# Feed-forward products of the prompt rows by Strassen's scheme, up phase before down phase

## The reference

```python
def _mlp(h, w_up, w_down):
    a = jnp.square(jax.nn.relu(jnp.einsum('bsd,df->bsf', h, w_up)))
    return jnp.einsum('bsf,fd->bsd', a, w_down)
# per layer: x = x + mixer(rmsnorm(x)) ; x = x + _mlp(rmsnorm(x), w_up, w_down)
```

## Time and profile before

| | |
|---|---|
| Median of 3 runs | 3071.8 us (3071.26 to 3075.94) |
| Profiled execution: time / span | 3069.31 / 3067.5 us |
| TensorE busy, products | 2958.7 us (96%) |
| TensorE busy, weight loads | 2498.5 us (81%) |
| VectorE, ScalarE, GpSimd busy | 1193.2, 907.5, 453.4 us |
| DMA | 165.91 MB, mean 54 GB/s |
| Mean granted TensorE clock | 0.987 |

### The profile page before, as it was taken

The page is one execution under the profiler, slowest core; times in us unless marked ns, Lnnn a source line. Parts: engine busy times, 40 slices in busy tenths (PEclk is TensorE's granted clock), DMA queues, the critical chain, the costliest instruction groups (busy, mean ns, idle before and its releaser), DMA issues.

```text
span 3067.5 us, 41859 instructions
## 1 busy us (share of the span) xinstructions
PE 2958.7 (96%) x16566; PEld 2498.5 (81%) x16566; DVE 1193.2 (39%) x2555; ACT 907.5 (30%) x1834; POOL 453.4 (15%) x283
## 2 busy tenths in 40 slices
...
DMA packets 146912, 165.91 MB, mean 54 GB/s; under 512 B 20032, under 2 KB 117600, under 8 KB 146784
## 3 DMA queue, kind: packets, MB, share of 16 engines
...
## 4 chain that ended last, share of the span: by engine, by line
PE 91%; DVE 5%; ACT 2%; issue 2%; POOL 1%; DMA 0%; ACTq 0%; SPq 0%; DVEq 0%; POOLq 0%
PE ps L1410 22%; PE ps L1408 22%; PE ps L1409 22%; PE ps L1550 6%; PE ps L1603 4%; PE ps L1580 4%; PE ps L1665 1%; PE ps L1522 1%; PE ps L1734 1%; PE ps L1420 1%; ACT pbuf L918 1%; DVE pbuf L1230 1%; POOL w_lo L698 1%; DVE pbuf L1198 1%; PE ps L1502 0%
## 5 line engine op out<-in xcount | busy, mean ns | idle before, releaser
L698 POOL TENSOR_TENSOR w_lo<-w_raw,w_hi 128x1024 fp32r<-128x1024 f32 (+2 forms) x158 | 376.4, 2383 | 2221.8 <-ACT w_hi L773 2221.8
L1408 PE MATMUL ps<-hT_hi,w_hi 128*128 128x384 f32 x1536 | 515.0, 335 | 4.8 <-DVE w_lo L1078 4.8
L1410 PE MATMUL ps<-hT_hi,w_lo 128*128 128x384 f32 x1536 | 514.6, 335 | 0.0
L1409 PE MATMUL ps<-hT_lo,w_hi 128*128 128x384 f32 x1536 | 514.4, 335 | 0.0
L1410 PE MATMUL ps<-w_hi,aT_lo 128*128 128x512 f32 x1152 | 448.4, 389 | 0.0
L1409 PE MATMUL ps<-w_lo,aT_hi 128*128 128x512 f32 x1152 | 448.4, 389 | 0.0
L1408 PE MATMUL ps<-w_hi,aT_hi 128*128 128x512 f32 x1152 | 448.1, 389 | 0.0
L1034 ACT ACTIVATE rbuf<-ps 128x384 f32<-128x384 f32 x192 | 94.5, 492 | 1140.9 <-PE ps L1410 1140.9
L1381 DVE TENSOR_TENSOR x<-ps,x 128x512 f32<-128x512 f32 x288 | 199.2, 692 | 560.2 <-PE ps L1410 560.2
L1373 DVE TENSOR_TENSOR rbuf<-rbuf 128x384 f32<-128x384 f32 x192 | 117.4, 612 | 577.1 <-ACT aT_hi L1036 577.1
L1408 PEld LDWEIGHTS ps<-hT_hi,w_hi 128*128 128x128 f32 x1536 | 289.4, 188 | 5.8 <-DVE w_lo L1078 5.3
...
## 6 DMA issues: line engine op xcount, KB each, us to landing
w_raw<-in_w_up_dram SPq DMA_DIRECT2D x64, 512.0 KB, 4.0
w_raw<-in_w_down_dram SPq DMA_DIRECT2D x64, 512.0 KB, 3.3
residual_scratch<-x SPq DMA_DIRECT2D x18, 512.0 KB, 7.7
x<-residual_scratch SPq DMA_DIRECT2D x18, 512.0 KB, 5.9
w_raw<-in_w_in_dram SPq DMA_DIRECT2D x16, 512.0 KB, 4.9
mixer_scratch<-omixT SPq DMA_DIRECT2D x16, 512.0 KB, 2.6
w_raw<-in_w_out_dram SPq DMA_DIRECT2D x16, 512.0 KB, 6.7
mixin<-mixer_scratch SPq DMA_DIRECT2D x16, 512.0 KB, 9.0
```

Source lines behind the costliest of these rows:

```text
L698: nc.gpsimd.tensor_tensor(w_lo[slot][:, 0:w], raw[i % 2][:, 0:w], w_hi[slot][:, 0:w], ALU.subtract).then_inc(lo_done.sem, 1)
L1408: pe.matmul(out, ah, bh, start=(k == 0), stop=False)
L1409: pe.matmul(out, ah, bl, start=False, stop=False)
L1410: last = pe.matmul(out, al, bh, start=False, stop=(k == n - 1))
```

## The change

Only the feed-forward changes (and, in its layout alone, the buffer of h for the other stages). The 8 x 8 grid of work over 1024 prompt rows is cut in halves in each dimension, and each of the 2x2 block products is made with Strassen's scheme in Winograd's form: 7 products of half size in place of 8, on sums and differences of the quarters of both operands. The 128 stream rows are multiplied in full.

- The layer first makes all hidden features (8 up turns), stores them in DRAM (`hidden_scratch`), and then makes all 8 down turns, loading them back. x goes to `residual_scratch2` before the up phase and is loaded back for the down phase, because T2, T3 and T4 (differences of the quarters of h, made once a layer) lie in its place.
- An up turn takes 256 features of each half. Its eight weight operands are the quarters 11, 12, 21, 22 and the sums S1 to S4, formed by VectorE, rounded by ScalarE, subtracted by GpSimd, in four slots. Its units (0, 1, 2, 3, 4, 6, 7) accumulate in PSUM; between them ScalarE copies partial results from PSUM to `cq`, VectorE adds the others to them, and squares with relu in one instruction. Four stream parts multiply 128 columns each.
- A down turn has nine weight operands (quarter 22 twice, and T1 to T4 formed by GpSimd) and eight hidden operands (the stream rows, quarters, S1 to S4 formed by VectorE), rounded by ScalarE; GpSimd makes the low parts of the weights, VectorE those of the hidden operands (`down_a_low`). TensorE makes first the stream products, then units 1 to 7, each in two pairs of tiles; VectorE adds each pair of banks (128 x 1024) into x, some results into two places by later units.
- `x_done` now tells of tiles 0 to 3, 4 and 5, and 6 to 8 only at the last two units of the last down turn.

The core of the diff (12 columns of indentation taken off; ScalarE's list and the T sums left out):

```diff
-FSLAB = 512
-NSLAB = FF // FSLAB
+NS = 8
+FB = FF // 2 // NS
...
+UP_OPS = ("11", "12", "S2", "S1", "S3", "21", "22", "S4")
+UP_END = (2, 5, 7, 9, 11, 12, 15, 17)
+UP_FREED_BY = (4, 5, 6, 7, 1, 1, 2, 3)
+UP_MM, UP_EV, UP_ADD = 17, 9, 3
...
+DN_B = ("22", "12", "11", "21", "T2", "T1", "T3", "22", "T4")
+DN_A = ("11", "12", "S1", "S2", "S3", "S4", "22")
+B_SLOT = (0, 1, 2, 3, 4, 0, 1, 2, 4)
+A_SLOT = (0, 1, 3, 2, 0, 1, 2)
+DN_MM = DN_EV = 15
...
-return dn_ev.at(l * NSLAB, 2 * (t + 1) - 18)
+return dn_ev.at(l * NS, (0 if t == NPT else 12 + t // 2) - DN_EV)
...
+    def down_turn(s):
+        T = l * NS + s
+        sp.wait_ge(a_lo.sem, a_lo.at(T, 1))
+        sp.wait_ge(a_out[4].sem, a_out[4].at(T, 32))
+        load(ras[:], as_d[s + 1], a_in[4])
+        sp.wait_ge(b_form.sem, b_form.at(T, 1))
+        sp.wait_ge(b_lo.sem, b_lo.at(T, 3))
+        load_down("11", s + 1)
+        sp.wait_ge(a_form.sem, a_form.at(T, 3))
+        sp.wait_ge(a_lo.sem, a_lo.at(T, 2))
+        for q in (0, 2):
+            sp.wait_ge(a_out[q].sem, a_out[q].at(T, 32))
+            load(ra[q][:], a_d[s + 1, q], a_in[q])
+        sp.wait_ge(b_form.sem, b_form.at(T, 3))
+        load_down("12", s + 1)
+        sp.wait_ge(b_form.sem, b_form.at(T, 4))
+        load_down("21", s + 1)
+        sp.wait_ge(a_form.sem, a_form.at(T, 4))
+        sp.wait_ge(a_out[1].sem, a_out[1].at(T, 32))
+        load(ra[1][:], a_d[s + 1, 1], a_in[1])
+        sp.wait_ge(b_lo.sem, b_lo.at(T, 8))
+        load_down("22", s + 1)
+        sp.wait_ge(a_lo.sem, a_lo.at(T, 8))
+        sp.wait_ge(a_out[3].sem, a_out[3].at(T, 32))
+        load(ra[3][:], a_d[s + 1, 3], a_in[3])
...
+    def down_low(T, o):
+        pool.wait_ge(b_hi.sem, b_hi.at(T, o + 1))
+        k = B_SLOT[o]
+        nc.gpsimd.tensor_tensor(wq_lo[k][:], down_b_source(o)[:], wq_hi[k][:],
+                                ALU.subtract).then_inc(b_lo.sem, 1)
+    def down_sums_12(T, s):
+        W = 2 * NS * l + NS + s
+        for q in (0, 1):
+            pool.wait_ge(wr_in[q].sem, wr_in[q].at(W, 16))
+        nc.gpsimd.tensor_tensor(bsum[0][:], rq[1][:], rq[0][:], ALU.subtract).then_inc(b_form.sem, 1)
+        pool.wait_ge(wr_in[3].sem, wr_in[3].at(W, 16))
+        pool.wait_ge(b_form.sem, b_form.at(T, 1))
+        nc.gpsimd.tensor_tensor(bsum[1][:], rq[3][:], bsum[0][:], ALU.subtract).then_inc(b_form.sem, 1)
+    def down_sum_3(T):
+        pool.wait_ge(b_lo.sem, b_lo.at(T, 6))
+        pool.wait_ge(b_form.sem, b_form.at(T, 2))
+        nc.gpsimd.tensor_tensor(bsum[0][:], rq[3][:], rq[1][:], ALU.subtract).then_inc(b_form.sem, 1)
+    def down_sum_4(T, s):
+        pool.wait_ge(b_lo.sem, b_lo.at(T, 5))
+        pool.wait_ge(wr_in[2].sem, wr_in[2].at(2 * NS * l + NS + s, 16))
+        nc.gpsimd.tensor_tensor(bsum[1][:], rq[2][:], bsum[1][:], ALU.subtract).then_inc(b_form.sem, 1)
...
+        down_low(T0, 0)
+        down_low(T0, 1)
+        down_low(T0, 2)
+        pool.wait_ge(up_mm.sem, up_mm.at(T, UP_END[4]))
+        down_sums_12(T0, 0)
+        down_low(T0, 3)
+        down_low(T0, 4)
...
+    def down_turn(T, s, last):
+        down_low(T, 5)
+        down_sum_3(T)
+        down_sum_4(T, s)
+        down_low(T, 6)
+        down_low(T, 7)
+        down_low(T, 8)
+        if not last:
+            down_low(T + 1, 0)
+            down_sums_12(T + 1, s + 1)
+            for o in range(1, 5):
+                down_low(T + 1, o)
...
+    def up_block(T, unit, copied, first_bank, q, k):
+        dve.wait_ge(up_mm.sem, up_mm.at(T, unit))
+        dve.wait_ge(up_ev.sem, up_ev.at(T, copied))
+        nc.vector.tensor_tensor(cq[q][:], bank(first_bank, 2), cq[q][:], ALU.add).then_inc(up_add.sem, 1)
+        dve.wait_ge(up_add.sem, up_add.at(T, k))
+        square(cq[q])
...
+    def down_a_low(T, o):
...
+        k = A_SLOT[o - 1]
+        nc.vector.tensor_tensor(sa_lo[k][:].rearrange("p k n -> p (k n)"), down_a_source(o - 1)[:],
+                                sa_hi[k][:].rearrange("p k n -> p (k n)"), ALU.subtract
+                                ).then_inc(a_lo.sem, 1)
...
+    def down_sums_12(T):
+        for q in (2, 3):
+            dve.wait_ge(a_in[q].sem, a_in[q].at(T, 16))
+        nc.vector.tensor_tensor(asum[0][:], ra[2][:], ra[3][:], ALU.add).then_inc(a_form.sem, 1)
+        dve.wait_ge(a_in[0].sem, a_in[0].at(T, 16))
+        dve.wait_ge(a_form.sem, a_form.at(T, 1))
+        nc.vector.tensor_tensor(asum[1][:], asum[0][:], ra[0][:], ALU.subtract).then_inc(a_form.sem, 1)
+    def down_sums_34(T):
+        dve.wait_ge(a_lo.sem, a_lo.at(T, 4))
+        dve.wait_ge(a_form.sem, a_form.at(T, 2))
+        nc.vector.tensor_tensor(asum[0][:], ra[0][:], ra[2][:], ALU.subtract).then_inc(a_form.sem, 1)
+        dve.wait_ge(a_in[1].sem, a_in[1].at(T, 16))
+        dve.wait_ge(a_lo.sem, a_lo.at(T, 5))
+        nc.vector.tensor_tensor(asum[1][:], ra[1][:], asum[1][:], ALU.subtract).then_inc(a_form.sem, 1)
+    def up_turn(T, s, first, last):
...
+        up_block(T, UP_END[0] + 2, 2, 4, 0, 1)
+        up_block(T, UP_END[3], 6, 2, 2, 2)
+        if not last:
+            dve.wait_ge(up_lo.sem, up_lo.at(T, 8))
+            up_sums_12(T + 1, s + 1)
+        dve.wait_ge(up_ev.sem, up_ev.at(T, 8))
+        square(cq[3])
+        dve.wait_ge(up_ev.sem, up_ev.at(T, 9))
+        square(cqs)
+        if last:
+            down_a_low(T0, 0)
+            down_a_low(T0, 1)
+            down_a_low(T0, 2)
+            down_sums_12(T0)
+        up_block(T, UP_END[7], 4, 2, 1, 3)
...
+    def evict(T, unit, pair, after):
+        half, t0 = ((0, 0), (0, 0), (1, 0), (1, 4), (1, 4), (1, 0), (0, 4))[unit - 1]
+        b0 = 4 if unit in (1, 3, 5, 7) else 0
+        dve.wait_ge(dn_mm.sem, dn_mm.at(T, 2 * unit + pair))
+        if after:
+            dve.wait_ge(dn_ev.sem, dn_ev.at(T, 2 * after + pair))
+        t = t0 + 2 * pair
+        part = x[:, t:t + 2, half * 512:(half + 1) * 512]
+        nc.vector.tensor_tensor(part, bank(b0 + 2 * pair, 2).rearrange("p (t n) -> p t n", t=2), part,
+                                ALU.add).then_inc(dn_ev.sem, 1)
+    def down_turn(T, last):
+        dve.wait_ge(dn_mm.sem, dn_mm.at(T, 1))
+        nc.vector.tensor_tensor(x[:, NPT, :], bank(0, 2), x[:, NPT, :], ALU.add).then_inc(dn_ev.sem, 1)
+        for unit in range(1, 8):
+            for pair in range(2):
+                evict(T, unit, pair, (0, 1, 0, 0, 4, 3, 0)[unit - 1])
+            if unit <= 3:
+                down_a_low(T, 4 + unit)
+            if last:
+                continue
+            if unit == 3:
+                down_a_low(T + 1, 0)
+            if unit == 4:
+                dve.wait_ge(a_lo.sem, a_lo.at(T, 8))
+                down_sums_12(T + 1)
+            if unit == 5:
+                down_a_low(T + 1, 1)
+            if unit == 6:
+                down_a_low(T + 1, 2)
+                down_a_low(T + 1, 3)
+            if unit == 7:
+                down_a_low(T + 1, 4)
+                down_sums_34(T + 1)
...
+    UNITS_UP = {0: (0, "11", True), 1: (4, "21", True), 2: (0, "T2", False), 3: (2, "T1", True),
+                4: (0, "T3", False), 6: (0, "T4", False), 7: (2, "22", False)}
+    def up_part(T, unit, fb, inc):
+        b0, name, new = UNITS_UP[unit]
+        wh, wl = wq_hi[unit % 4], wq_lo[unit % 4]
+        h, lo_h = H_HI[name], H_LO[name]
+        out = bank(b0 + fb)
+        for k in range(4):
+            cols = slice(k * FB + fb * P, k * FB + (fb + 1) * P)
+            pe.matmul(out, wh[:, cols], h[:, k, :], start=new and k == 0, stop=False, skip_group_check=True)
+            pe.matmul(out, wh[:, cols], lo_h[:, k, :], start=False, stop=False, skip_group_check=True)
+            last = pe.matmul(out, wl[:, cols], h[:, k, :], start=False, stop=k == 3, skip_group_check=True)
+        if inc:
+            last.then_inc(up_mm.sem, 1)
...
+        stream_part(0, 0, 0)
+        stream_part(1, 0, 4).then_inc(up_mm.sem, 1)
...
+    def down_products(out, ah, al, bh, bl, new, final):
+        for k in range(2):
+            pe.matmul(out, ah[:, k, :], bh[:, k * 512:(k + 1) * 512], start=new and k == 0, stop=False,
+                      skip_group_check=True)
+            pe.matmul(out, ah[:, k, :], bl[:, k * 512:(k + 1) * 512], start=False, stop=False,
+                      skip_group_check=True)
+            last = pe.matmul(out, al[:, k, :], bh[:, k * 512:(k + 1) * 512], start=False,
+                             stop=final and k == 1, skip_group_check=True)
+        return last
+    UNITS_DN = {1: (4, 1, 2, True), 2: (0, 2, 3, True), 3: (4, 4, 4, False), 4: (0, 3, 5, True),
+                5: (4, 5, 6, False), 6: (0, 6, 7, False), 7: (4, 7, 8, False)}
+    def down_turn(T):
+        pe.wait_ge(a_lo.sem, a_lo.at(T, 1))
+        pe.wait_ge(dn_ev.sem, dn_ev.at(T, 12 - DN_EV))
+        for o, half, k0 in ((0, 1, 2), (1, 1, 0), (2, 0, 0), (3, 0, 2)):
+            pe.wait_ge(b_lo.sem, b_lo.at(T, o + 1))
+            last = down_products(bank(half), sas_hi[:, k0:k0 + 2, :], sas_lo[:, k0:k0 + 2, :], wq_hi[o],
```

(27 more changed lines are left out.)

662 lines of the change are left out of this document (497 added, 165 removed).

## The result

The changed kernel takes 3127.01 us (median of 4, 3124.41 to 3128.53) beside 3071.53 for the kernel before on the same chip: a ratio of 1.0177, 95% interval 1.0164 to 1.019. It is slower, by 55.5 us; 3148 had been predicted, in a range of 3070 to 3210. The profiled execution took 3127.43 us, its span is 3125.6.

The account below looks back on a forecast made before the run. TensorE's products were taken to bound the kernel. Two layers +47.0, the next layer's start +0.5 and the end +28.5 made +76 us on 3069.31, and 2.5 more for the median gave 3148 us; range 3070 to 3210.

Parts of the forecast that it names:

- The likeliest case: Whole kernel slower through engine waits in down turns, pause between phases and longer tail; 3125 to 3170 us, chance 45%.
- the two engines' meetings: Down turns: VectorE instruction with two SBUF inputs waits until GpSimd's instruction ends; 3.3 us amid a string of GpSimd work.
- the gap: Between up and down phases: down products wait for VectorE's last addition, queued behind low parts and sums; 11.7 us a layer.
- the end: After the last product: final norm at GpSimd's 4.58 us pace, VectorE ending at 32.6 instead of 4.1; +28.5 us.
- Start of the phase: Before the first up product: ScalarE's square and copy, then two VectorE steps come last; 4.4 us a layer.
- The up phase: Eight up turns of 48.9 us, helper engines hidden; 391.1 us a layer, plus 1.8 stage transposes and 1.7 clock.
- the eight down turns with their clock: First turn 44.2 us, seven more of 50.7: 399.1 a layer, plus 13.6 for lowered clock after waits.
- the walk: Settled down turn timed by VectorE's instructions: TensorE waits 2.3 us before unit 1, 4.8 before unit 2; turn 50.7.
- (a): Engine meetings cost nothing: pause between phases 4.1 us, down turns 43.6, one clock fall; 3008 us, faster; chance 15%.
- (b): Down turns: VectorE lets one more whole GpSimd instruction ahead; 53.6 us a turn, 3189 us in all; chance 21%.
- (c): TensorE's clock holds through the waits in down turns and between phases: 27 us less, 3121 us; chance 15%.
- (d): Up turns: 128-column stream products take 0.062 us each; 77 us less, 3071 us, no change; chance 4%.

Follow-up runs that it names:

- e4: Changed kernel with VectorE's last addition and squaring of the up phase moved ahead of low parts 1 and 2 and two sums: 3130.76 us.
- e6: Changed kernel with the edits of e3, e4 and e5 together: 3000.8 us, ratio 0.9775 to the kernel before.
- e9: Changed kernel with the e3 and e5 edits, VectorE's low parts and sums around the first down turn respread, last squaring right behind last addition: 3008.4 us.
- e2: Changed kernel with VectorE's low parts of hidden operands cut to 16 columns of 1024 in the down turns (output incomplete): 3022.02 us.
- e1: Changed kernel with GpSimd's low parts of the down weights cut to 16 columns of 1024 in the down turns (output incomplete): 3021.22 us.
- e3: Changed kernel with VectorE's sums S3 and S4 moved behind the eviction of the stream products, no work left out: 3029.57 us, ratio 0.9859.
- e5: Changed kernel with the final product with g_final on VectorE instead of GpSimd: 3107.07 us, ratio 1.0117 to the kernel before.

## Why the prediction was right, and where its sizes were off

The likeliest case, own chance 45%, came in: slower, by the two engines' meetings, the gap and the end. Its signs are there: 0.11 between stream products, turns over 50, a median of 2.6 us for VectorE's instructions of two SBUF inputs in a settled down turn, evictions at 1.21. Its sum was 21 us too high, and its own range of 3125 to 3170 just holds the time. Point by point, for layer 0:

- Start of the phase: 4.4 predicted, 4.43 measured (738.36 to 742.79). One reading of the earlier trace rows was wrong and did no harm: before the change TensorE did not stand from 742.9 to 747.43, eight transposes lie between (from 743.95), and its idle time was 1.1 and 2.39 us; the sum took only the 742.9. The up phase: 391.1 + 1.8 + 1.7 = 394.6, measured 395.5. The choice of 0.112 for stream products was right (0.11 apart); by the figure of the Trainium skill (TensorE: Matmul & The Clock Gate, Back-to-back issue gap) the phase would have been, by estimate, 24 us shorter, and the trace does not agree. The helpers hid in it, as said.
- The gap: 11.7 predicted, 11.93 measured in both layers. `e4`, `e6` and `e9` show it as VectorE's work ahead of the last addition.
- The mechanism of the down turns was right: `e2` shows the waiting, `e1` what a turn is without it, `e3` the instruction it passes through. The Trainium skill (SBUF — State Buffer, Who interferes with whom) says the same of two SBUF inputs, and the 0.16 against 1.53 us of `e2` agrees with it.
- **The term that was mis-sized** is the eight down turns with their clock: 399.1 + 13.6 = 412.7 predicted, 401.1 measured. A settled turn was to be 43.6 + 2.3 (before unit 1) + 4.8 (before unit 2) + 1.7 of clock = 52.4. Measured from start to start it is 43.5 + 0.3 + 4.4 + 1.7 of clock in the second turn, and the clock's part grows to 3.0 in the last: 50.0 to 51.2. Two errors of opposite sign stand in it. The waits were too high by 17 us a layer, 14 of them before unit 1; the clock after the waits of the seven turns was too low by 7 (11.9 counted, 18.6 measured). That they partly cancel is luck: with the clock alone sized right, the sum would have been 13 us further off. In all it is 11.6 us a layer, 23 for both.
- Why the wait before unit 1 was not there: VectorE left its evictions of the turn before at 1192.8, 2.4 us ahead of the turn and not 0.2. Its own account of a settled turn (1395.42 to 1446.49) is 30.7 of work, 15.3 in eight waits for GpSimd and 5.1 idle; the walk had 32.4, 16.4 in nine waits and 1.9. Its instructions without a meeting start 1.13 us apart when they stand back to back (1209.54, then 1210.67 above), where the walk counted 1.22 each. The step that failed is thus the walk of VectorE, one meeting too many and each unhindered instruction too long.
- Why the clock cost more: the lower level lasted 6.8 us and not 3.4 in turns three to eight; there it began during the wait, and it ended later and later into unit 2, at 1214.5 in the second turn and 1521.7 in the last (3.7 and 6.0 us after unit 2 began). The wait before unit 2 kept its 4.4 us in all seven turns, and each turn is longer by what the clock took; VectorE, which then waits for TensorE (4.0 us idle in the second turn, 5.1 in a settled one), does not make that up. No run changed the clock alone, and why the stretch grows is open.
- The next layer's start: +0.5 predicted, +1.2 measured (its third transposes come 16.7 us after the last product, 15.5 before). The end: 28.5 predicted, 27.6 measured (31.7 less 4.1), and `e5` shows GpSimd's pace as its cause.
- Together: 13.0 and 13.7 for the layers (812.9 and 813.6 against 799.9), 1.2, 27.6: 55.5, the difference of the medians. The two spans differ by 58.1; the rest lies in stages that were not changed, 3.4 us less in layer 0's mixer and 6.1 more in layer 2's, where the clock was at its lower level for 6.8 us less and 17 us more.

Of the rivals, (a), meetings that cost nothing, fails by the 4.28 us waits; yet its price of a turn, 43.6, is what `e3` nearly reaches with five sixths of the waiting in the meetings still there. (b), a worse order, (c), a clock that holds (0.54 is shown after the waits), and (d), stream products at 0.062, fail by the rows shown.

So where did the saved products go? TensorE's list is 102 us shorter by the working of the prediction. Against that stand 62 us of waits before unit 2, 37 of the clock behind them, 4 of the waits before unit 1, 3 of clock in the first down turns, 24 in the two gaps and 29 at the next layer's start and the end: 159, a loss of 57, beside 55.5 by the medians and 58.1 by the two spans.
